# An expert layer's outputs collected on chip: slot table, indirect row loads and 0/1 matrix products in place of a round trip through memory

## The reference

```python
def hier_moe(h, wg, bg, we, be, w1, w3, w2):
    pg = softmax(hf @ wg + bg);  gsel = argmax(pg);  pg_sel = max(pg)          # 4 groups
    le = (hf @ we + be) of the chosen group                                     # 8 experts in it
    p_top, e_loc = top_k(softmax(le), 2)
    gate = pg_sel[:, None] * p_top / sum(p_top)
    ...
    def expert_block(args):
        xb, e = args
        return (silu(xb @ w1[e]) * (xb @ w3[e])) @ w2[e]
    ys = ys * gate_buf[:, None]
    out = zeros((n + 1, d)).at[tok_buf].add(ys)[:n]

x = x + hier_moe(h2, ...)
```

## Time and profile before

| | |
|---|---|
| median of 3 runs | 1492.77 us (1492.45 to 1495.0) |
| profiled execution, its own time | 1491.96 us |
| its span, first to last instruction | 1490.2 us |
| mean granted TensorE clock | 0.991 |
| TensorE busy | 1427.3 us (96%) |
| VectorE, ScalarE, GpSimd busy | 521.9, 423.3, 34.2 us |
| transfers | 313.88 MB, mean 211 GB/s |
| chain of work that ended last | PE 88%, DMA 5%, DVE 4%, ACT 2% |

### The profile page before, as it was taken

The page is one execution under the profiler, slowest core; times in us unless marked ns, Lnnn a source line. Parts: engine busy times, 40 slices in busy tenths (PEclk is TensorE's granted clock), DMA queues, the critical chain, the costliest instruction groups (busy, mean ns, idle before and its releaser), DMA issues.

```text
span 1490.2 us, 16715 instructions
## 1 busy us (share of the span) xinstructions
PE 1427.3 (96%) x6940; PEld 905.5 (61%) x6940; DVE 521.9 (35%) x942; ACT 423.3 (28%) x732; POOL 34.2 (2%) x84
## 2 busy tenths in 40 slices
PE   5999999799999999999999799999999999999998
PEld 4777775485454445445444354555457888887886
DVE  4224556735311212121221226276234322223324
ACT  4124765613100000000200242165333222223232
POOL 0000110000000000000000201000000000000000
PEclk9999999899999999999999999999999999999999
DMA  9841118425999999999999732100005133222201
GB/s 346 275 195 57 57 59 318 161 98 241 387 428 427 428 427 428 428 428 426 428 427 427 302 128 104 57 0 1 0 11 213 59 113 113 78 92 114 85 0 57
DMA packets 30197, 313.88 MB, mean 211 GB/s; under 512 B 3908, under 2 KB 3908, under 8 KB 12456
## 3 DMA queue, kind: packets, MB, share of 16 engines
q1 hardware_dynamic: 22456, 295.54, 48.3%
q10 hardware_dynamic: 6512, 13.06, 2.8%
q0 software_dynamic: 1152, 4.19, 0.8%
HBM read 298.35 MB, written 14.43 MB: 210 GB/s over the span
## 4 chain that ended last, share of the span: by engine, by line
PE 88%; DMA 5%; DVE 4%; ACT 2%; issue 1%; POOL 0%; SPq 0%; ACTq 0%; DVEq 0%; POOLq 0%
PE ps L55 84%; DMA ring<-in_w 4%; PE ps L1131 2%; DMA ring<-in_w_in 1%; PE ps L872 1%; POOL B L549 0%; DMA B<-yslots,SMI 0%; DVE TMP L1934 0%; PE ps L612 0%; PE ps L794 0%; DVE X L1723 0%; PE ps L833 0%; DVE UL L1720 0%; ACT TMP L1647 0%; DVE TMP L1723 0%
## 5 line engine op out<-in xcount | busy, mean ns | idle before, releaser
L55 PE MATMUL ps<-ring,B 128*64 128x512 f32 (+2 forms) x880 | 230.0, 593 | 6.2 <-DMA ring<-in_w 4.6
L55 PEld LDWEIGHTS ps<-ring,B 128*64 128x64 f32 (+1 forms) x880 | 79.3, 146 | 132.4 <-issue 126.6
L55 PE MATMUL ps<-XH,WH 128*128 128x512 f32 (+1 forms) x368 | 141.1, 383 | 1.3 <-DVE XL L1720 0.7
L55 PE MATMUL ps<-B,B 128*128 128x128 f32 (+1 forms) x1072 | 140.0, 291 | 0.4 <-DVE B L1989 0.4
L55 PE MATMUL ps<-XL,WH 128*128 128x512 f32 (+1 forms) x368 | 139.9, 380 | 0.0
L55 PE MATMUL ps<-XH,WL 128*128 128x512 f32 (+1 forms) x368 | 139.9, 380 | 0.0
L55 PEld LDWEIGHTS ps<-B,B 128*128 128x128 f32 (+1 forms) x1072 | 121.8, 190 | 25.8 <-issue 24.2
L55 PE MATMUL ps<-B 128*64 128x512 f32 (+5 forms) x440 | 114.5, 554 | 0.0
L1629 ACT ACTIVATE WH<-ring 128x2048 fp32r<-128x2048 f32 x33 | 63.2, 1916 | 167.8 <-PE ps L55 167.8
L1720 DVE TENSOR_TENSOR WL<-ring,WH 128x2048 fp32r<-128x2048 f32 x33 | 75.7, 2293 | 94.7 <-ACT WH L1629 94.7
L1460 ACT ACTIVATE TMP<-ps 64x512 f32<-64x512 f32 x32 | 19.0, 593 | 212.0 <-PE ps L55 212.0
(11 more groups left out here) (299 smaller groups left out, 2018.2 us busy)
## 6 DMA issues: line engine op xcount, KB each, us to landing
ring<-in_w SPq DMA_DIRECT2D x65, 2048.0 KB, 21.6
B<-in_w SPq DMA_DIRECT2D x24, 2048.0 KB, 19.9
ring<-in_w_ada SPq DMA_DIRECT2D x12, 2048.0 KB, 8.6
ring<-in_w_gu SPq DMA_DIRECT2D x11, 2048.0 KB, 8.1
ring<-in_w_in SPq DMA_DIRECT2D x7, 2048.0 KB, 12.5
TO<-in_w SPq DMA_DIRECT2D x7, 2048.0 KB, 19.8
ring<-in_w_down SPq DMA_DIRECT2D x5, 2048.0 KB, 7.2
yslots<-TMP ACTq DMA_DIRECT2D x64, 128.0 KB, 8.5
```

What stands on the lines that cost most here:

```text
L55: return e.matmul(o, l, r, start=first, stop=last, skip_group_check=True)
```

## The change

- Each (token, choice) has a place in a table of 64 x 48 entries in memory (`tdram`): the token's number and its gate. It is first filled with "nobody" and 0 (one write on the ScalarE queue in place of the 15 zero tiles); GpSimd scatters 8 times 128 entries of 8 bytes into it, and ScalarE reads it back twice (one copy for each half of the partitions) at its step x = 1.
- The normed tokens are also written to memory (`xndram`, 2 MB, SyncE). From the third pair on a pair's tokens come by an indirect load of 128 rows of 4 KB (rows of nobody are skipped, so the buffer is set to 0 first) and 8 turns of 128x128 (`turn_in`) in place of the 32 products.
- The output of an expert stays on chip: ScalarE takes it out of PSUM times the gate in the fp32r format (YH), VectorE forms the rest (YL), VectorE builds a 0/1 matrix of 64 (twice) x 512 (`rows_of`), TensorE multiplies both into four banks for each quarter k of the tokens (`combine`, 4 products of 64 rows for each k), and VectorE adds them to X (`added`, two additions of 128x512 for each k). `combine(x-2, .)` stands inside the products of x, at c = 2, 3, 5 and 6.
- `yslots`, its writes and the 8 loads behind the experts are gone. The passes add to X through the same kind of product. The context's keys come behind the passes, between the turns of X; on ScalarE the norms, the turned rows and the keys' copies stand in a new order.

```diff
@@ sync
+        e.wait_ge(h2n, 4)
+        e.dma_start(xndram.rearrange("(t p) n -> p t n", p=128), xn).then_inc(xn_out, 16)
         for i in range(I_EXP + 8, i0):
...
-        for k in range(2):
-            e.wait_ge(y_out[k], NE * 16)
+        e.wait_ge(dn_mm2, NE)
         passes(sp_pass)(e)
         e.nop().then_inc(ov_done, 1)
-        e.wait_ge(xo, 8)
         load(i0)
@@ gpsimd
         e.wait_ge(si_set, 1)
-        e.wait_ge(gate_set, 1)
-        e.wait_ge(ov_done, 1)
+        e.wait_ge(gate_set, 2)
         for k in range(4):
             for j in range(2):
-                e.indirect_dma_start(out=GB[2 * k + j], out_offset=None, in_=ydram,
-                                     in_offset=bass.IndirectOffsetOnAxis(ap=SI[:, j, k:k + 1], axis=0)).then_inc(gb_in[2 * k + j], 16)
+                e.indirect_dma_start(out=tdram, out_offset=bass.IndirectOffsetOnAxis(ap=SI[:, j, k:k + 1], axis=0),
+                                     in_=SRC[:, k, j, :], in_offset=None).then_inc(tbl_out, 16)
+        e.wait_ge(idx_set, 2)
+        e.wait_ge(xn_out, 16)
+        for p in range(2, NE // 2):
+            e.wait_ge(ga_mm, 2 * p - 2)
+            e.memset(XG[p % 2], 0.0).then_inc(xg_zero, 1)
+            e.wait_ge(xg_zero, p - 1)
+            e.indirect_dma_start(out=XG[p % 2], out_offset=None, in_=xndram, in_offset=..., bounds_check=511, oob_is_err=False).then_inc(xg_in[p % 2], 16)
@@ tensor
+        def turn_in(p):
+            e.wait_ge(xg_in[p % 2], 16 * (p // 2))
+            e.wait_ge(ga_xt, 2 * p)
+            e.wait_ge(cm_add, 8 * (2 * p - 2))
+            for n in range(2):
+                for q in range(4):
+                    c = 4 * n + q
+                    t = e.transpose(P[n][:, 128 * q:128 * q + 128], XG[p % 2][:, 128 * c:128 * c + 128], ident)
+                t.then_inc(ga_mm, 1)
+
+        def banks_of(y, k):
+            return (0, 1) if k % 2 else (5, 6 + y % 2)
+
+        def combine(y, k):
+            if k == 0:
+                e.wait_ge(row_set, y + 1)
+                e.wait_ge(yl_set, y + 1)
+                if y in (24, 25):
+                    e.wait_ge(cT_dve, 4 * (y - 23))
+                if y:
+                    e.wait_ge(cm_add, 8 * y - 2)
+            elif k > 1 or y:
+                e.wait_ge(cm_add, 8 * y + 2 * k - 2 if k > 1 else 8 * y)
+            for w, first in ((YH, True), (YL, False)):
+                for h in range(2):
+                    m = mm(e, P[banks_of(y, k)[h]], OHT[y % 2][64 * h:64 * h + 64, 128 * k:128 * k + 128], w[64 * h:64 * h + 64, :], first, not first)
+            m.then_inc(cm_mm, 1)
...
                 for c in range(8):
+                    if x >= 2 and c in (2, 3, 5, 6):
+                        combine(x - 2, (2, 3, 5, 6).index(c))
                     if c == 4 and x:
                         turn(x - 1)
...
             else:
                 turn(x - 1)
+                for k in range(4):
+                    combine(x - 2, k)
-            if x % 2 == 1 and x + 1 < NE:
-                gather(x // 2 + 1)
+            if x == 1:
+                gather(1)
+            elif x % 2 == 1 and x + 1 < NE:
+                turn_in(x // 2 + 1)
...
+        for k in range(4):
+            combine(NE - 1, k)
+        e.wait_ge(si_set, 1)
+        passes(pe_pass)(e)
+        e.wait_ge(ov_done, 1)
@@ scalar
+            if x == 1:
+                e.wait_ge(tbl_out, 128)
+                for h in range(2):
+                    e.dma_start(MISC[64 * h:64 * h + 64, 0:2 * NCOL], tdram.rearrange("(s n) w -> s (n w)", s=CAP)).then_inc(tbl_in, 16)
+                e.wait_ge(tbl_in, 32)
             if x >= 1:
                 y = x - 1
...
-                e.activation(YS[y % 2], P[6 + y % 2], ACT.Copy).then_inc(ys_cp, 1)
-                e.wait_ge(ys_cp, y + 1)
-                for h in range(2):
-                    e.dma_start(ydram[CAP * y:CAP * y + CAP, 512 * h:512 * h + 512], YS[y % 2][64 * h:64 * h + 64, :]).then_inc(y_out[y % 2], 16)
+                e.activation(YH[:, :], P[6 + y % 2], ACT.Copy, scale=TAB[:, y, 1:2]).then_inc(yh_set, 1)
...
+        row_norm(0)
+        row_norm(1)
+        e.wait_ge(cx_mm, 1)
+        e.activation(LW[:, 0:256], P[2][:, 0:256], ACT.Square).then_inc(cx_act, 1)
+        turned_rows(0)
...
+        row_norm(2)
+        turned_rows(1)
+        row_norm(3)
         turned_rows(2)
+        for m in range(4):
+            e.activation(KB[2 * m + 1][0:64, 0:256], ..., ACT.Copy).then_inc(cx_act, 1)
         turned_rows(3)
@@ vector
+        step(e.scalar_tensor_tensor(out=wide, in0=rank, scalar=float(NCOL), in1=ov, op0=ALU.mult, op1=ALU.add))
+        step(e.scalar_tensor_tensor(out=wide, in0=tj, scalar=float(1 - CAP * NCOL), in1=wide, op0=ALU.mult, op1=ALU.add))
+        step(e.tensor_copy(SI, wide))
+        for k in range(4):
+            step(e.tensor_scalar(place_of[:, 128 * k:128 * k + 128], iota, 128.0 * k, None, ALU.add))
+        def added(y, k):
+            e.wait_ge(cm_mm, 4 * y + k + 1)
+            ...
+            for h in range(2):
+                xs = X[:, k, 512 * h:512 * h + 512]
+                e.tensor_tensor(xs, P[((0, 1) if k % 2 else (5, 6 + y % 2))[h]], xs, ALU.add).then_inc(cm_add, 1)
+        def rows_of(y):
+            e.tensor_scalar(OHT[y % 2][:, :], place_of, TAB[:, y, 0:1], None, ALU.is_equal).then_inc(row_set, 1)
+        def y_low(y):
+            e.wait_ge(yh_set, y + 1)
+            times(YL[:, :], P[6 + y % 2], TAB[:, y, 1:2], YH[:, :], ALU.subtract).then_inc(yl_set, 1)
...
+            for k in range(4):
+                if k == 2 and x >= 1:
+                    hidden_cols(x - 1)
+                if x >= 2:
+                    added(x - 2, k)
             if x < NE:
                 hidden(x)
-            if x % 2 == 0 and x + 2 < NE:
-                one_hot(x // 2 + 1)
+            if x == 0:
+                one_hot(1)
...
+            if x == 1:
+                e.wait_ge(tbl_in, 32)
+                for h in range(2):
+                    r = slice(64 * h, 64 * h + 64)
+                    e.tensor_copy(IDX[r, :], TAB[r, h:NE:2, 0]).then_inc(idx_set, 1)
+            if x >= 1:
+                rows_of(x - 1)
+                y_low(x - 1)
```

More of the change, by code:

```diff
@@ L106, in body @@
     P = [ps[:, b, :] for b in range(8)]
-    ydram = nc.dram_tensor("yslots", (NTILE * CAP, 1024), F32, kind="Internal").ap()
+    tdram = nc.dram_tensor("table", (CAP * NCOL, 2), F32, kind="Internal").ap()
+    xndram = nc.dram_tensor("xnormed", (512, 1024), F32, kind="Internal").ap()
     bdram = nc.dram_tensor("biasrow", (4, 640), F32, kind="Internal").ap()
@@ L209, in body @@
     HT = [TMP[:, 1536 + 256 * k:1792 + 256 * k].rearrange("p (f n) -> p f n", f=4) for k in range(2)]
-    YS = [TMP[:, 2048 + 512 * k:2560 + 512 * k] for k in range(2)]
+    YH, YL = again("YH", [128, 512], "TMP", 2048), again("YL", [128, 512], "TMP", 2560)
+    XG = [TMP[:, 3072:4096], B2[:, 0:1024]]
+    OHT = [again(f"OHT{k}", [128, 512], "B23", 1024 + 2560 * k) for k in range(2)]
+    TAB = MISC[:, 0:2 * NCOL].rearrange("p (n w) -> p n w", w=2)
+    SRC = MISC[:, 96:112].rearrange("p (t j w) -> p t j w", t=4, j=2)
+    gate = SRC[:, :, :, 1].rearrange("p t j -> p j t")
+    IDX = SMI[:, 12:28]
+    place_of = LW[:, 0:512]
     hcT = TO[:, 0:2048].rearrange("p (c n) -> p c n", c=8)
@@ L241, in body @@
     TX = TMP[:, 2048:2304].rearrange("p (f n) -> p f n", f=4)
-    cell = small[0:1, 57:59]
+    cell = small[0:1, 57:58]
     cmpx = small[0:1, 0:32]
     basex = small[:, 60:61]
-    icell = SMI[0:1, 9:11]
-    GB = [B3[:, 1024 * k:1024 * k + 1024] for k in range(8)]
+    icell = SMI[0:1, 9:10]
+    OGX, OGT = TMP[:, 2816:3072].rearrange("p (t n) -> p t n", t=4), TMP[:, 3072:3584]
     jc = TMP[:, 0:1024]
@@ L400, in body @@
     again_ = iter(spent)
[L401 removed]
     ft_in, rope_in, out_done = (next(again_) for n in ("ft_in", "rope_in", "out_done"))
[L403 removed]
+    xo_act, xo_T, hT_dve, hT_act = (next(again_) for n in ("xo_act", "xo_T", "hT_dve", "hT_act"))
     qa_mm, qa_act, qa_dve, qn_mm, kv_mm, kr_act, kvn_act, kvn_mm, kvn_dve = (
@@ L563, in pe_pass @@
             m = acc(e, P[0][:, 64 * c:64 * c + 64], [(xn[:, i, 128 * c:128 * c + 128], OX[0][:, i, :]) for i in range(4)])
+        m.then_inc(ov_pe, 1)
+        for k in range(4):
+            for d in range(2):
+                m = mm(e, P[5][64 * d:64 * d + 64, 128 * k:128 * k + 128], OGX[:, k, :], ident, True, True)
         m.then_inc(ov_pe, 1)
@@ L931, in small_keys, with turn_x @@
             return m
+        def turn_x(k):
+            b = 0 if k % 2 == 0 else 6
+            e.wait_ge(xo_act, 4 * k + 4)
+            if k == 0:
+                e.wait_ge(cm_add, 8 * NE)
+            if k >= 2:
+                e.wait_ge(hT_dve, 4 * k - 4)
+                e.wait_ge(hT_act, 4 * k - 4)
+            for h in range(2):
+                for q in range(4):
```

(2 more changed lines are left out.)

188 lines of the change are left out of this document (94 added, 94 removed).

## The result

The changed kernel takes 1517.4 us (median of 4 runs, 1516.17 to 1521.98); the kernel before took 1492.61 beside it. The ratio is 1.017, with a 95% interval of 1.0157 to 1.0183: slower by 24.8 us, 1.7%, small but clear of noise, where I had forecast 12.9 (10.9 + 2; the 1505 us that I named lie 12.4 above 1492.61).

What follows compares the result with a forecast made beforehand. TensorE and the weight transfers were taken as nearly level bounds in the experts' stage. 1491.96 (profiled) + 10.9 at the experts' end + 2 behind gave 1504.9, predicted as 1505 us; range 1488 to 1526, the forecast's own 1499 to 1513.

Steps and rivals of the forecast that it cites:

- The pair: TensorE's step for two experts: gather out -6.36, groups +6.0, waits +0.2; -0.2 us, called 0, over 15.5 pairs.
- the stall: Start of the experts' stage: TensorE waits 12.6 us for the table's way through memory, plus 1.9 cold clock.
- the end of the waits for weights: Experts' stage: TensorE's waits for late weight loads, with the clock behind them, go; -6.4 us.
- The experts' end: End of the experts' stage: +10.9 us by TensorE, which decides over +6.6 by the loads.
- Steps 25 and 26: Late experts' steps, where the context's columns stand before y_low on VectorE: +2.5 us.
- Behind the experts: From the last turn to the query products: +2 us, ends -4 and +7, with ScalarE as the chain.
- TensorE reads the count and does the context's products, 4.7 us, until 21: Behind the experts, once X is whole: products take 4.7 us, ending 21 us after the last turn.
- My 34.5: Behind the experts: query products start 34.5 us after the last turn, before 32.5; ScalarE's copies end at 34.4.
- SiLU: Experts' stage on TensorE: the later SiLU of the first expert adds 0.3 us.
- The faster one: Rival: relief of the transfers is what is left, needing the table at about 396; 1487 to 1488 us; chance 0.22.
- Slow scatters: Rival at the start: scatters slow by themselves, table at 420, 13 us more than the sum, 1518; chance 0.12.
- Groups not side by side: Rival: fp32r halves don't run side by side (or VectorE's additions hold groups up); +3.4 a pair, 1558; chance 0.08.

Runs made afterwards that it cites:

- old_gather: Kernel changed with all experts' rows gathered again by one-hot products instead of indirect loads and turns, the new sum kept; 1609.73 us (single run).
- merged: Kernel changed with an expert's four groups in two places of the block, two back to back, banks of even and odd k exchanged; 1507.18 us.
- table_ready: Kernel changed with the table in use written by VectorE with fixed entries, so no reading back at the start; 1506.11 us.
- no_branch: Kernel changed without the passes for overfull experts on any engine, so nothing branches behind the experts; 1510.25 us.
- short_body: Kernel changed with the passes' body on TensorE cut to two instructions, a wait and a clear, the branch kept; 1511.24 us.
- shift_100: Kernel changed with 100 empty, semaphore-signalling instructions on TensorE in its wait for the table, moving the leap's place in the code; 1514.91 us.
- on_chip_table: Kernel changed with the table of slots formed on chip by eight f32 products, without scatters, table in memory or reading back; 1508.84 us.
- full_array: Kernel changed with each group as two products of 128 rows in place of four of 64 (x gets a wrong sum); 1520.9 us.
- tail_moved: Kernel changed with table on chip, groups in two places, and the context's products moved into TensorE's gaps; 1486.69 us, ratio 0.9956 to the kernel before.

## Why the prediction was wrong in size

The pair, the stall and the end of the waits for weights stood where I had forecast them; one term of the sum was too small, one was missing (the leap), and several smaller ones were off.

**The experts' end, +10.9 forecast, +15.4 measured.** Count by turns. From the first turn (0) to the last (31) the kernel before takes 455.85 us and the changed one 472.65, 16.8 more; the first turn is 1.4 earlier.
- *The pair, "which I call 0": +10.8.* This is the step that failed most here. A block with an expert's four groups costs 3.31 us more than without (an even step 14.17 for 10.85, turn to turn), and a gather replaced gives 6.32. The pair is therefore +0.30 and not -0.16. And the two don't come in equal number: up to the last turn the groups of 30 experts stand (99.3 us), but only 14 gathers go (88.5), the first two pairs being gathered as before. By my own prices 15 pairs of groups against 14 gathers were +4.0 already: I multiplied a pair by 15.5 instead of counting each kind. The other 6.8 are the price, above all that of a group with its share of the wait for YL: 0.83 instead of the 0.775 (6.2 / 8) of the sum, 120 times, is 6.3. old_gather (6.3 for each gather) and merged (1.39 less for a pair, with four changes fewer) bear out both prices.
- *The stall, 12.6 + 1.9 forecast: 9.5 + 2.6.* Scatters landed at 393.06, not 402, and the table at 401.4, not 407; in other executions the stall is up to 1.8 us longer. The total of table_ready agrees: 11.3 less.
- *Waits for weights, -6.4:* they went; by the balance, what is left when the other terms are taken off, they and the clock behind them were 7.8. The merged kernel, where they come back, shows how near the loads are.
- *Steps 25 and 26, +2.5:* +0.4 there (turn 24 to 27 takes 48.12 us, of which 44.8 are plain steps and some 2.9 the context's columns, which the kernel before has too), but +1.3 one step earlier, which I had not looked for: before the additions of step 24 VectorE waits 3.46 us for ScalarE and then scales the context's rows for 1.42 (from 734.15), and the group at 736.82 waits for those additions. Turn 23 to 24 takes 15.44 us in place of 14.16. Together +1.7.
- *Ahead of the experts, 0:* -1.4, within what single executions differ by.
- 12.1 + 10.8 + 1.7 - 7.8 = 16.8; minus 1.4 is 15.4.

**Behind the experts, +2 forecast, +8.7 measured.** This is the other failed step: "TensorE reads the count and does the context's products, 4.7 us, until 21". The leap over the passes' body left TensorE idle for 5.6 us. no_branch, short_body and shift_100 give 34.7, 35.0 and 34.6 us where the kernel changed has 41.2, so the leap is 6.2 to 6.6 of the 8.7. A stretch of cold clock that costs about 2 us is in all of them, on one group of products or another behind the last turn; it isn't the leap's doing, as the expectation of no_branch had it. The kernel before has such a stretch too (0.51 granted in 855 to 860). My 34.5 held none, and I had made ScalarE's norms the chain; in no_branch the context's products and the first turns of X are it, on TensorE:

```profile
868.01 7.38 PE ps L57 x51
```

So that 34.7 meets 34.5 is in part luck. I had named late code behind the branch as an end of the range (+7), but gave the branch nothing in the sum: 17.7 less 1.4 for the last two additions, plus 4.7 for the products, is 21 already.

In the kernel before two things kept the leap out of sight: it stood at a cheap place in the code (0.34 us for the branch, 5.99 after), and beside a wait of 6.80 us for ScalarE. The change took both away. Either would have been enough or nearly: a cheap leap with nothing to cover it is 1.3 us from register load to next product (shift_100, whose 34.6 us are no more than no_branch's 34.7), and a dear one from 849.70 would have ended at 855.7, about when ScalarE let TensorE go on at 855.44 (an estimate from those rows; not run).

**The size in one line:** pairs 10.8 and tail 6.7 over the forecast, 6.3 under it in the smaller terms (1.4 ahead of the experts, 2.4 stall and clock, 0.3 SiLU, 0.8 steps 24 to 26, 1.4 waits for weights); 12.9 + 11.2 = 24.1. The forecast's direction held, and the wide range (1488 to 1526); its own range, 1499 to 1513, did not.

**The rivals.** The faster one needed the table at 396: it came at 401.4, and even with it at hand (on_chip_table) the kernel is slower than before, since TensorE and not the loads is the bound. Slow scatters: no. Groups not side by side: no, by full_array.

**What stays open.** That the place of the leap decides is shown by two kernels moved on purpose, one in each direction, and agrees with all others. From the first to the last of queue 8's 54 packets the trace has 13,242 instructions of TensorE, and some 310 are leapt over: 256 for each packet, an estimate. Counted modulo 256 in the built program (the trace's own count is 18 less in every run), leaps of some 310 instructions were dear from 191, 192, 200 and 223 and cheap from 35, 40 and 60; the leap of the kernel before, over a body of 60 products, was cheap from 22, and shorter ones (171 and 11) from 191 were cheap. That the cause is a further block of code not yet at hand is the reading that fits, with the packets; it is not shown, and where the edges lie was not tried.

## What to carry to other kernels

Count added and removed pieces each by its own number over the whole loop, before pairing them off: two costs that cancel in a step need not come equally often. Where a loop that seldom runs is leapt over, read the duration of the branch itself before and after the change, and ask what stood beside it: a leap over a few hundred instructions took TensorE 0.3 us or 6, by where in the code it fell, and any change ahead of it moves it. Short products in another layout are cheapest back to back, since of the 0.80 us of a group 0.35 are the change there and back.

## What the runs showed of the hardware that I had not expected

- Leaving 128*64 products for a group and coming back costs 0.35 us, the same for 64*128 and 128*128 groups.
- TensorE's leap over 76 products takes 1.2 to 1.3 us from the register load to the next product, or 6.8 to 7.5 with a packet of instructions arriving in between (4.5 with no other transfers on the way). The branch itself takes 0.34 to 0.44 us, or 6.0 to 6.6 (3.6).
- Empty instructions with a semaphore's signal are not free on TensorE: 40 took 6.0 us, 0.15 each.
- Eight scatters of 8-byte entries beside weight loads (381 GB/s in 376 to 393): 7.3 us from the last issue to all landed; two reads of 24 KB, 8.3 us from the first issue.
- A TensorE kept waiting for weights in short stretches, busy for 82.13 of 100 us, was granted 0.95 of its clock. Behind the last turn, with idle stretches of 0.9 to 6.8 us, a stretch of products ran at half the clock in every profile read for it, the kernel before and tail_moved included: 3.60 us of products took 5.52 (no_branch), 4.72 took 6.92 or 7.46 (short_body, the kernel changed), 1.89 took 3.63 (tail_moved).
